# Weight copies, gate units and one output pair rearranged in a three-layer fp32 mixer kernel

## The reference, cut to what matters

```
for layer in (0, 1):
    h = rmsnorm(x, norm_g[layer])
    if layer == 0:   # gated convolution and attention, 8 heads
        y_a = silu(layernorm(conv(u_val * sigmoid(u_gate)))) * silu(z_a)
        y_b = attention(q_b, k_b, v_b) * silu(z_b)
        y = concat(y_a, y_b)
    else:            # compressed/selected/window attention, and banded attention
        y_c = nsa_attention(...) * silu(z_c)
        y_d = banded_attention(...) * silu(z_d)
        y = concat(y_c, y_d)
    x = x + y @ w_out[layer]
# second block: retention and dilated attention, gated merge, then a ReLU^2 MLP
x = x + g1 * token_mixer(modulate(rms_norm(x)))
x = x + g2 * (square(relu(modulate(rms_norm(x)) @ w_ff1)) @ w_ff2)
return rms_norm(x)
```

## Time and profile before

| | |
|---|---|
| time, median of 3 runs | 964.17 us (960.16 to 964.74) |
| time of the profiled execution | 960.53 us |
| its span | 958.7 us |
| mean granted TensorE clock | 0.989 |
| PE busy, share of the span | 96% |
| POOL busy, ACT busy, DVE busy | 61%, 44%, 38% |

### The profile page before, as it was taken

How to read it: one execution, slowest core, us unless ns; L and a number is a source line. 1 busy time by engine, 2 the same in 40 slices (tenths; PEclk the granted TensorE clock), 3 DMA queues, 4 the chain that set the end, 5 groups by cost and what they waited for, 6 DMA issues and landing times.

```text
span 958.7 us, 16460 instructions
## 1 busy us (share of the span) xinstructions
PE 919.5 (96%) x6922; PEld 845.5 (88%) x6922; DVE 366.8 (38%) x758; ACT 423.1 (44%) x610; POOL 588.8 (61%) x457
## 2 busy tenths in 40 slices
PE   6999999799899999999999999999999999999997
PEld 5888778798776889988999789999999799999997
DVE  3987563220888348400111113312124455540001
ACT  2112373336665423344434355767334455553430
POOL 0000064475500428998686777677799879999880
PEclk9999999799999999999999999999999999999998
DMA  9743447658152655755444444535546735554521
GB/s 346 308 137 127 187 177 257 233 187 318 54 177 101 251 212 197 263 178 179 154 151 162 145 166 142 175 133 175 186 167 245 326 136 182 191 194 158 192 92 44
DMA packets 27905, 177.60 MB, mean 185 GB/s; under 512 B 3080, under 2 KB 5780, under 8 KB 7480
## 3 DMA queue, kind: packets, MB, share of 16 engines
q1 hardware_dynamic: 26248, 174.35, 50.1%
q10 hardware_dynamic: 1584, 2.20, 0.7%
HBM read 174.95 MB, written 3.43 MB: 186 GB/s over the span
## 4 chain that ended last, share of the span: by engine, by line
PE 89%; DVE 4%; ACT 3%; DMA 2%; issue 1%; POOL 1%; ACTq 0%; DVEq 0%; SPq 0%
PE proj L678 16%; PE proj L681 16%; PE proj L680 16%; PE proj L653 10%; PE proj L711 5%; PE proj L758 3%; PE proj L761 3%; PE proj L760 3%; DMA raw<-in_weights 2%; PE proj L1002 1%; PE proj L729 1%; PE mixed L905 1%; PE scores L862 1%; PE proj L1022 1%; PE mixed L888 1%
## 5 line engine op out<-in xcount | busy, mean ns | idle before, releaser
L597 POOL TENSOR_TENSOR w_lo<-raw,w_hi 128x512 fp32r<-128x512 f32 (+1 forms) x316 | 405.0, 1317 | 192.7 <-ACT w_hi L1278 192.5
L680 PE MATMUL proj<-parts,w_lo 128*128 128x256 f32 x840 | 237.7, 283 | 0.4 <-POOL w_lo L597 0.4
L678 PE MATMUL proj<-parts,w_hi 128*128 128x256 f32 x792 | 227.6, 287 | 0.4 <-ACT arena L1303 0.2
L681 PE MATMUL proj<-parts,w_hi 128*128 128x256 f32 x792 | 223.9, 283 | 0.0
L1278 ACT ACTIVATE w_hi<-raw 128x2048 fp32r<-128x2048 f32 (+2 forms) x79 | 149.2, 1891 | 118.0 <-PE proj L681 55.7
L680 PEld LDWEIGHTS proj<-parts,w_lo 128*128 128x128 f32 x840 | 161.1, 192 | 1.4 <-issue 0.7
L678 PEld LDWEIGHTS proj<-parts,w_hi 128*128 128x128 f32 x792 | 151.7, 192 | 2.0 <-issue 1.1
L681 PEld LDWEIGHTS proj<-parts,w_hi 128*128 128x128 f32 x792 | 151.6, 191 | 0.0
L597 POOL TENSOR_TENSOR w_lo<-arena,w_hi 128x512 fp32r<-128x512 f32 x36 | 47.1, 1341 | 141.9 <-ACT w_hi L1278 141.9
L711 PE MATMUL proj<-parts,w_hi 128*128 128x256 f32 x288 | 54.8, 288 | 9.8 <-POOL w_lo L597 7.6
L711 PEld LDWEIGHTS proj<-parts,w_hi 128*128 128x128 f32 x288 | 46.6, 196 | 12.0 <-issue 10.9
(11 more groups left out here) (320 smaller groups left out, 2077.5 us busy)
## 6 DMA issues: line engine op xcount, KB each, us to landing
raw<-in_weights SPq DMA_DIRECT2D x109, 1024.0 KB, 4.9
arena<-in_weights SPq DMA_DIRECT2D x39, 1024.0 KB, 5.1
probT<-in_weights SPq DMA_DIRECT2D x8, 1024.0 KB, 5.8
dil_lines<-dil_line SPq DMA_DIRECT2D x1, 2304.0 KB, 14.1
raw<-in_weights SPq DMA_DIRECT2D x3, 512.0 KB, 6.4
dil_bias<-dil_lines SPq DMA_DIRECT2D x1, 1536.0 KB, 9.5
xT<-in_x SPq DMA_DIRECT2D x2, 512.0 KB, 6.0
arena<-in_alibi SPq DMA_DIRECT2D x1, 1024.0 KB, 20.5
```

Source lines behind the costliest of these rows:

```text
L597: nc.gpsimd.tensor_tensor(lo_slots[RAW_AT[n]][:, at], raw_slots[RAW_AT[n]][:, at], hi_slots[HI_AT[m]][:, at].bitcast(F32), ALU.subtract).t ...
L678: nc.tensor.matmul(dst, whi, h, start=first, stop=False)
L680: nc.tensor.matmul(dst, wlo, h, start=False, stop=False)
L681: last = nc.tensor.matmul(dst, whi, lo[:, k, :], start=False, stop=stop)
```

## The change

1. `kskw` may be copied one group earlier, and `output_squares(0, ...)` calls `passing` once more in front of `root`, for units up to `kskw`. The layer-1 h is kept in `h_one` (in `dil_bias`) in place of `wide`, and `two_units` asks for a unit's low parts only when it comes to it.
2. `zc0`, `zc1`, `zd0`, `zd1` leave `SPLIT`: they are multiplied whole, from `h_one`. POOL's clearing of `probT` moves behind the last layer-1 unit, which is where it stood in POOL's order.
3. The gate `za1` is made by one Silu on ACT in place of tanh and a DVE product; its place on ACT is behind the high copy of y piece 2.
4. The pair `wo0_0`, `wo0_1` begins with piece 2 as a fill of the last unit (`B:wo0`), ahead of the last mix. The high copy of piece 0 comes in front of the last of the four Silus, and DVE makes its low part at once.
5. `ad11a`, `ad11b` are loaded behind `f1_3` in place of in front of `f1_2`.

```
-FILL_B = [... , "ad1 L:scale")]
+FILL_B = [... , "ad1 B:wo0 L:scale")]
-SPLIT_SOON = [... "kd", "zc0", "zc1", "zd0", "zd1"]
+SPLIT_SOON = [... "kd"]
-                     (("ad10a", "ad10b", "ad11a", "ad11b"), "f1_2")):
+                     (("ad10a", "ad10b"), "f1_2"), (("ad11a", "ad11b"), "f1_4")):
+        h_one = cut(dil_bias[:].rearrange("p g h j -> p (g h j)")[:, 0:KD * S], S)
# POOL
-                if u == "zc0":
+                if u == "rq0":
                     pool.wait_ge(proj_ready, GROUP_AT["hidv"] + 1)
                     nc.gpsimd.memset(probT[:, 0:512], 0.0)...
# PE: two_units(names, stretches, pair=None, done=True)
-                banks = [begin(name) for name in names]
-                units = [(UNITS_OF[name][0], *weight(UNITS_OF[name][0])) for name in names]
+                        if fresh:
+                            pair["banks"][i] = begin(name)
+                        w = weight(u)
+                elif name == "B:wo0":
+                    pe.wait_ge(pt_ready, rounds_before(PART["b"][-1] + 1))
+                    state["pair"] = two_units(("wo0_0", "wo0_1"), convolved(0, 1), done=False)
+                src = h_one if src is None and name not in SPLIT_AT else src      # in chunk
...
-                    two_units(("wo0_0", "wo0_1"), [... all four pieces ...])
+                    two_units(("wo0_0", "wo0_1"), convolved(1, 4), state["pair"])
# ACT
-                    loaded = LOADED_AFTER[v] + 1 if v in SPLIT_SOON else ...
+                    loaded = LOADED_AFTER[v] + (v != "kskw") if v in SPLIT_SOON else ...
                 elif name == "L:scale":
-                    between("za1")
                     convolved_high(Y_ORDER[0])
+                    copy_out("za1", tmp[:, 1], fn=ACT.Silu)
                     act.wait_ge(sem("ln_scaled"), 1)
                     for c in range(4):
+                        if c == 3:
+                            convolved_high(Y_ORDER[1])
                         nc.scalar.activation(..., ACT.Silu, ...)
...
+                if layer == 0:
+                    passing("kcvc", SPLIT_AT["kskw"] + 1)
                 root(stream)
# DVE, conv_end
-                gate_out("za1")
                 parts_low(yT0, Y_ORDER[:1])
                 for c in range(2):
...
+                    if c == 0:
+                        V.scalar_tensor_tensor(two(yT0, c), y, 0.5, tmp[:, c], ALU.mult, ALU.mult)...
+                        parts_low(yT0, Y_ORDER[1:2])
+                    else:
+                        V.tensor_tensor(two(yT0, c), y, tmp[:, c], ALU.mult)...
-                parts_low(yT0, Y_ORDER[1:3])
...
-            parts_low(yT0, Y_ORDER[3:])
+            parts_low(yT0, Y_ORDER[2:])
```

More of the change, by code:

```diff
@@ L55 @@
     [[f"av{g}"] for g in range(AG)]
-FILL_B = [x.split() for x in ("zb1 ad0 L:mean E:zb0", "za0 L:sq E:zb1 E:ad0 L:centre", "za1 E:za0 L:var", "ad1 L:scale")]
+FILL_B = [x.split() for x in ("zb1 ad0 L:mean E:zb0", "za0 L:sq E:zb1 E:ad0 L:centre", "za1 E:za0 L:var", "ad1 B:wo0 L:scale")]
 FILL_CD = [x.split() for x in (
@@ L148, in last_in @@
     return [g for g in BANKED[:FILL_AT[group]] if BANK_OF[g] == b][-1]
-SPLIT_SOON = [f"wo0_{i}" for i in range(4)] + ["kcvc", "kskw", "vsvw", "qc0", "qc1", "vdgt", "qd0", "qd1", "kd", "zc0", "zc1", "zd0", "zd1"]
+SPLIT_SOON = [f"wo0_{i}" for i in range(4)] + ["kcvc", "kskw", "vsvw", "qc0", "qc1", "vdgt", "qd0", "qd1", "kd"]
 SPLIT = [u for u in WEIGHTS if u in SPLIT_SOON or WEIGHT_AT[u] >= WEIGHT_AT["rq0"] and u[:2] != "ad"]
@@ L510, in half_gates @@
         def half_gates():
-            return [f"{n}{i}" for n in ("zb", "za", "zc", "zd") for i in range(2)]
+            return ["zb0", "zb1", "za0"] + [f"{n}{i}" for n in ("zc", "zd") for i in range(2)]
         class Steps:
@@ L692, in project, with two_units @@
                 features(name, *h_parts, [[(u, P * j, 0)] for j in range(unit_shape(u)[1] // P)], wait)
-            def two_units(names, stretches):
-                banks = [begin(name) for name in names]
-                units = [(UNITS_OF[name][0], *weight(UNITS_OF[name][0])) for name in names]
-                first, last_one = [True, True], stretches[-1]
+            def two_units(names, stretches, pair=None, done=True):
+                pair = pair or dict(banks=[None, None])
                 for stretch in stretches:
                     ks, products, wait = stretch
-                    for i, (u, whi, wlo) in enumerate(units):
+                    final = done and stretch is stretches[-1]
+                    for i, name in enumerate(names):
+                        u = UNITS_OF[name][0]
+                        fresh = pair["banks"][i] is None
+                        if fresh:
+                            pair["banks"][i] = begin(name)
+                        w = weight(u)
                         for k in ks:
@@ L706, in two_units, with convolved @@
                             for j in range(2):
-                                at = slice(P * j, P * j + P)
-                                for w, part in products:
-                                    if w:
+                                for low, part in products:
+                                    if low:
                                         second_half(u, k)
[L711 to L714, removed]
+                                    last = nc.tensor.matmul(pair["banks"][i][:, S * j:S * j + S], w[low][:, k, P * j:P * j + P],
+                                                            parts[:, part, k, :], start=fresh,
+                                                            stop=final and (k, j, (low, part)) == (ks[-1], 1, products[-1]))
+                                    fresh = False
+                        if final:
                             end(last)
+                return pair
+            every = ((0, 0), (1, 0), (0, 1))
+            def convolved(lo, hi):
+                return [((2 * c, 2 * c + 1), every, lambda k, n=n: pe.wait_ge(y_ready, n + 1)) for n, c in enumerate(Y_ORDER) if lo <= n < hi]
             def project_two(names, n):
@@ L1671, in stream_norm @@
                 for k in range(KD):
-                    V.scalar_tensor_tensor(wide[:, S * k:S * k + S], xT[:, k, :], gain[:, k:k + 1], spread, ALU.mult, ALU.mult) \
-                        .then_inc(h_full, 1)
+                    V.scalar_tensor_tensor(full(k), xT[:, k, :], gain[:, k:k + 1], spread, ALU.mult, ALU.mult).then_inc(h_full, 1)
                 for k in range(KD):
```

17 lines of the change are left out of this document (8 added, 9 removed).

## The result

| | before | after |
|---|---|---|
| time, median of 6 runs each | 963.56 us (960.16 to 964.74) | 947.1 us (944.73 to 948.65) |
| time of the profiled execution | 960.53 us | 944.73 us |
| its span | 958.7 us | 942.7 us |
| mean granted TensorE clock | 0.989 | 0.998 |

After over before is 0.9834, with a 95% interval of 0.981 to 0.9857: faster by 16.0 us (13.8 to 18.3). The forecast was 945.0 in a range of 939.5 to 951, and the sum for the profiled execution 943.4 against 944.73. The profiled execution after is the fastest of its six, with the highest clock. The other five have clocks of 0.994 to 0.996 and spans of 943.8 to 946.7.

What follows compares the result with a forecast made beforehand. PE was taken to bound the kernel: busy 96% of the span, 89% of the ending chain. Terms 9.6 + 1.9 + 1.5 + 4.1 = 17.1 us off the profiled execution gave 943.4; 1.6 above that, 945, range 939.5 to 951.

Steps and rivals of the forecast that it cites:

- Part 1: Layer 1's norm: early `kskw` copy starts the pair 7.5 us earlier and saves 2.1 of low clock, 9.6 in all.
- that `two_units` asks for each unit in turn: Pair `kcvc`, `kskw`: PE needs `kskw` only at 170.5, its low part being ready by 167.9, after a start at 166.7.
- The lower sum by the Trainium skill's rule: Ahead of layer 1's norm: POOL on `kskw`'s low part blocks DVE up to 1.4 us; sum 15.7 instead of 17.1.
- Parts 3 and 4: End of the first attention: Silu gate and early pair gain 1.7 us, up to 2.3; 1.9 taken.
- piece 0 better placed: End of the first attention: piece 0 better placed in time raises the gain from 1.7 up to 2.3 us.
- Part 2: Second attention: whole gate units take away 4.7 us against 3.2 of unhidden added PE work, a gain of 1.5.
- 4.7 taken away: Second attention: 2.3 us of DVE contention, 0.8 from an earlier tanh and 1.6 of low clock go.
- the 1.6 booked for it: Second attention: the next half unit takes 2.95 us warm instead of 4.54 at clock 0.62, 1.6 gained.
- The rival with the gate units' whole cost: Second attention: PE still stands, the clock falls, 4.9 us added with at most 1.7 hidden; 948, chance 0.11.
- Part 5: Norm before the MLP: `f1_2` and `f1_3` land earlier, so sums, clock and first products gain 4.1 us.
- The fear that the wait would move to `ad11`: Norm before the MLP: loads share the queue, PE waits for `ad11` instead, no gain there; 947.5, chance 0.08.
- The allowance of 1.6 between the sum and the median: Whole kernel: forecast set 1.6 us above the sum, since the median before lay 3.6 above the profiled time.

Runs made afterwards that it cites:

- ask_both: The changed kernel, with PE again waiting for the first half of both units' low parts ahead of the pair's first product; 946.49 us, ratio 0.9859.
- pool_busy: The changed kernel plus eight POOL subtractions of 128x256 that nobody reads, from the second attention's first transposes on; 946.46 us, ratio 0.9838.
- squares_first: The kernel before, with ACT's squares for `wo2_2` and `wo2_3` at the third norm ahead of the unit copies, loads unchanged; 959.82 us, ratio 0.9979.
- tanh_gate: The changed kernel with `za1` again by tanh and a DVE product, in front of piece 2's high copy; span 948.7 us, one run.
- pair_after_mix: The changed kernel with the pair `wo0_0`, `wo0_1` begun only after the last mix, Silu kept; 945.64 us, one run.
- gates_split: The changed kernel with all four gate units `zc0`, `zc1`, `zd0`, `zd1` split again; 946.78 us, ratio 0.9851.
- ad11_first: The changed kernel with `ad11a` and `ad11b` loaded ahead of `f1_2` again; 951.21 us, ratio 0.9902.
- copy_late: The changed kernel with `kskw`'s high copy back behind layer 1's high parts, units still asked for one by one; 951.38 us, ratio 0.9896.
- lines_first: The changed kernel with the 2.3 MB broadcast `dil_lines` issued ahead of `kskw`'s load instead of behind it; 954.54 us, one run.

## Why the prediction was right

**Part 1** was sized right: 7.5 for the start and 2.1 for the clock, 9.6 in all; measured 7.4 and 2.2. The first 80 products took 9.63 us, and the window of after that answers to the standstill of the earlier trace rows has a granted clock of 1.00:

```profile
168.00:172.00 4.00, 4.00 (x37) 4.00 (x36) 3.13 (x11) 1.33 (x1) 2.60 (x2) 1.00 1.01 422
```

One sentence of its working fell away: that `two_units` asks for each unit in turn gave nothing here, since `kskw`'s low part was done at 165.68, not at 167.9, and the pair starts at 164.91; ask_both loses nothing. The lower sum by the Trainium skill's rule (SBUF — State Buffer, Who interferes with whom), 15.7 for POOL blocking DVE under `kskw`'s low part, was not borne out at this place: that low part ran until 165.68, DVE's eight products for h, which read only x as a tile in SBUF and the spread sums in PSUM, and so are not the case that the rule names, went on at 0.40 us each from 163.84, and its low parts, with two operands in SBUF, began at 166.97 only, when POOL had finished. Where two such operands did meet POOL the runs agree with the rule: in pool_busy the instruction that came second waited, on either engine, and in squares_first DVE's did (numbers above and below).

**Parts 3 and 4** were 1.9 and measured 1.5. The steps as told came in time: PE started piece 2 at 133.17, for which 133.8 stood. But the weight put on them was wrong: tanh_gate and pair_after_mix show that the whole gain is that of Silu and its place (1.6), and that the early pair is worth 0.0. The term is 0.4 too large, and its "piece 0 better placed" brought nothing beyond it.

**Part 2** was 1.5 and measured 0.6. Its two halves, read from the same traces. In the first pair of row tiles (first scores to the products after the fourth half unit, 238.36 to 264.24 before, 226.86 to 249.85 after) 2.9 was gained, where the working had 4.7 taken away less 1.2 of added work, 3.5. The wait of 2.57 went down to 0.30 and that of 0.56 to 0.26, 2.6 in place of 3.1 for contention and the earlier tanh together; the DVE rows are as predicted:

```profile
239.11 0.16 DVE L1778 TENSOR_TENSOR stat<-stat,arena 128x4 f32<-128x4 f32 x1
239.31 0.69 DVE L1780 TENSOR_TENSOR wide<-wide,stat 128x512 f32<-128x512 f32 x1
```

The clock did not fall in the profiled execution (the halves in question took 4.61 and 3.08 us before, 3.61 and 3.62 after). But the 1.6 booked for it was too large, and this is the term of the sum that was mis-sized. gates_split has the same wait and kept a clock of 1.00 behind it, so it shows what the clock alone gives: 25.4 us over this pair against 25.9 before. Only 0.5 is gained, because the next probabilities come no sooner: the low part of `zd1` lies under them in both, and PE waits 1.23 for them in gates_split. The whole units brought the other 2.4, and gates_split also shows that split ones do not always make the clock fall. In the rest 2.3 was lost where 1.9 was reckoned: four halves at 0.5 each and 0.4 more of waits around the first of them, less the wait of 0.47 that went; that makes 2.0, and 0.3 lies in overlaps between rows. The rival with the gate units' whole cost named a clock that still falls. It does in some executions of the kernels derived from it, at other waits; that this is why the median stands above the profiled execution is likely and not shown, since only the fastest one was profiled.

**Part 5** was 4.1; 3.9 and 4.1 were measured (stage table, ad11_first). The fear that the wait would move to `ad11` did not come true: PE has no wait for a load there.

**The sum** was 17.1 for the profiled execution and 15.8 came, 16.0 of span: part 2 is 0.9 of the difference, parts 3 and 4 are 0.4, part 5 is 0.2, 0.2 lies outside the span, and 0.3 was gained ahead of any change. The allowance of 1.6 between the sum and the median was a guess. It was too small by about 0.8, since the profiled execution was the fastest of six. Between medians the forecast was a gain of 19.2 (964.17 to 945) and 16.5 came (963.56 to 947.1): the sum foretold the profiled execution better than its 945 foretold the median.

## What to carry to other kernels

A standstill that recurs with an in-order engine waiting for a load is found in that engine's timeline and not in the share of busy time; moving one copy of 1.9 us ahead of a norm, across 7.5 us of waiting, gave 9.6 of the 16 us. When work is moved ahead of a wait, look which queue entry stands in front of its load, and what another engine will be doing under the work that now comes earlier: in squares_first 2.8 of 3.5 us went back to two engines meeting in SBUF. Taking work from a helper engine by giving PE more paid here only where that helper's work lay under a chain that PE waits for: `zd0` whole did, while the variants that left `zc0` and `zc1` split were 1.2 and 1.6 us shorter over that stretch.

## What the runs showed of the hardware that I had not expected

- **A POOL instruction delays a DVE product that starts inside it, by up to its own length.** DVE's low part of h (128x256, both operands in SBUF) takes 0.47 us at its fastest. In squares_first, with POOL at 128x512 subtractions of 1.3 us throughout, its median is 1.50 and its longest 1.52. With POOL instructions of 0.73 us the 128x4 product took 0.39 us more. The other way round, a POOL instruction that started behind a DVE product took 1.26 in place of 0.73. Products of DVE for h at 163.84, which read the spread sums, ran at 0.40 us each beside POOL. But two SBUF operands are not the only case: in pool_busy a 128x4 TENSOR_SCALAR with one (246.25) took 0.64 in place of 0.16, and ended as POOL did.
- **The granted clock falls after the same short waits in some executions and not in others.** The kernel after has a wait of 1.83 us at 274.2 and the clock stays at 1.00; pair_after_mix, gates_split and pool_busy have the same wait and then 0.69, 0.69 and 0.67 over 4 us, at a cost of 1.1 to 1.4 us. All fourteen profiled kernels have this wait, and the clock fell behind it in seven: tanh_gate, copy_late, lines_first and ad11_first are the others. pool_busy also fell to 0.57 at 228 to 232, before its POOL work began and with the same PE work as after up to there; after did not. Single runs of one kernel differ by 0.9 (copy_late's four) to 5.1 us (ask_both's), and parts of 1 us are told apart only by distances inside a trace, with its clock falls taken off. What decides when it falls stays open.
- **A load's time depends on what was issued ahead of it.** 1 MB took 4.9 to 5.0 us with a 2.3 MB broadcast behind it and 12.0 us with the same broadcast issued 5.3 us ahead of it (lines_first, one run).
